# One-pass index products on stacked high and low parts in a one-core decoder step

## What is computed

```python
def _index_scores(qi, wi, ki):
    s = jnp.einsum('bthd,bsd->bths', qi.astype(jnp.float32), ki.astype(jnp.float32))
    scale = (IDX_DIM ** -0.5) * (IDX_HEADS ** -0.5)
    return jnp.einsum('bths,bth->bts', jax.nn.relu(s), wi.astype(jnp.float32)) * scale
...
def block(i):
    start = i * Q_BLOCK
    qib = lax.dynamic_slice_in_dim(qi, start, Q_BLOCK, axis=1)
    wib = lax.dynamic_slice_in_dim(wi, start, Q_BLOCK, axis=1)
    scores = _index_scores(qib, wib, ki)
    scores = jnp.where(causal[None], scores, -jnp.inf)
    _, idx = lax.top_k(scores, topk)
```

## Time and profile before

| | us |
|---|---|
| runs shown, median of 3 | 1151.43 |
| lowest, highest | 1148.69, 1152.35 |
| the profiled execution, its own time | 1152.24 |
| its span, first to last instruction | 1150.4 |
| TensorE busy | 1124.0 |
| VectorE, ScalarE, GpSimd busy | 641.1, 326.6, 374.1 |
| from the first index tile's matmuls to the first row score | 34.04 to 179.58 |

### The profile page before, as it was taken

The page is one execution under the profiler, slowest core; times in us unless marked ns, Lnnn a source line. Parts: engine busy times, 40 slices in busy tenths (PEclk is TensorE's granted clock), DMA queues, the critical chain, the costliest instruction groups (busy, mean ns, idle before and its releaser), DMA issues.

```text
span 1150.4 us, 29654 instructions
## 1 busy us (share of the span) xinstructions
PE 1124.0 (98%) x11836; PEld 1048.8 (91%) x11836; DVE 641.1 (56%) x1184; ACT 326.6 (28%) x605; POOL 374.1 (33%) x158
## 2 busy tenths in 40 slices
PE   7999999999999999999999999999999999999996
PEld 6888889999999999999999898988989889999994
DVE  3566667897547556754266564555546443233356
ACT  4333333323332322232232221221212332121340
POOL 1532332333234333433441313221322233433570
PEclk9999999999999999999999999999999999999997
DMA  8433242233233323335423888888978785232333
GB/s 264 121 102 88 81 103 75 77 102 84 74 93 100 81 81 92 84 83 167 116 61 116 279 307 283 308 280 275 331 244 298 224 289 139 73 91 81 105 108 156
DMA packets 208040, 175.87 MB, mean 153 GB/s; under 512 B 20114, under 2 KB 188874, under 8 KB 206706
## 3 DMA queue, kind: packets, MB, share of 16 engines
q1 hardware_dynamic: 194392, 165.58, 46.5%
q10 hardware_dynamic: 13538, 8.68, 2.7%
HBM read 164.29 MB, written 10.03 MB: 152 GB/s over the span
## 4 chain that ended last, share of the span: by engine, by line
PE 90%; DVE 5%; DMA 2%; issue 1%; SPq 0%; ACT 0%; DVEq 0%; ACTq 0%
PE acc L1180 66%; PE acc L1162 4%; PE acc L1595 3%; PE bank L1526 3%; PE bank L1281 2%; PE bank L1398 2%; PE acc L1648 2%; PE bank L1417 1%; DVE scoreP L1900 1%; PE acc L1252 1%; DMA xnat<-in_x_prompt 1%; DVE top L1896 1%; PE acc L1554 1%; PE bank L1333 1%; PE bank L1407 1%
## 5 line engine op out<-in xcount | busy, mean ns | idle before, releaser
L670 POOL TENSOR_TENSOR wL<-rawW,wH 128x1024 fp32r<-128x1024 f32 (+1 forms) x154 | 373.9, 2430 | 745.6 <-ACT wH L692 745.5
L1180 PE MATMUL acc<-actH,wH 128*128 128x272 f32 x2136 | 457.2, 295 | 0.0
L1180 PE MATMUL acc<-actH,wL 128*128 128x272 f32 x2136 | 441.9, 288 | 0.0
L1180 PE MATMUL acc<-actL,wH 128*128 128x272 f32 x2136 | 440.8, 288 | 0.0
L1180 PEld LDWEIGHTS acc<-actH,wH 128*128 128x128 f32 x2136 | 334.7, 188 | 30.1 <-issue 29.6
L1180 PEld LDWEIGHTS acc<-actL,wH 128*128 128x128 f32 x2136 | 335.8, 189 | 0.0
L1180 PEld LDWEIGHTS acc<-actH,wL 128*128 128x128 f32 x2136 | 333.8, 189 | 0.0
L692 ACT ACTIVATE wH<-rawW 128x1024 fp32r<-128x1024 f32 (+1 forms) x154 | 161.7, 1054 | 260.1 <-PE acc L1180 232.1
L1852 DVE SCALAR_TENSOR_TENSOR scoreP<-relu,wiN,scoreP 128x256 f32<-128x256 f32 (+2 forms) x54 | 45.4, 880 | 33.4 <-ACT relu L750 33.4
L2248 DVE SCALAR_TENSOR_TENSOR y<-y,bank 128x512 f32 x12 | 8.2, 688 | 89.0 <-PE bank L1715 87.0
L2005 DVE STREAM_TRANSPOSE kPage<-kPage 128x1024 f32<-128x1024 f32 x30 | 37.1, 1236 | 36.5 <-DMA kPage<-in_cache_k 35.8
(11 more groups left out here) (238 smaller groups left out, 1118.6 us busy)
## 6 DMA issues: line engine op xcount, KB each, us to landing
rawW<-in_w_in SPq DMA_DIRECT2D x112, 512.0 KB, 3.9
vPage<-in_cache_v SPq DMA_DIRECT2D x64, 512.0 KB, 6.9
kPage<-in_cache_k SPq DMA_DIRECT2D x60, 512.0 KB, 5.1
rawW<-in_w_out SPq DMA_DIRECT2D x40, 512.0 KB, 4.0
y<-in_x_prompt SPq DMA_DIRECT2D x4, 1024.0 KB, 7.8
out_y_prompt<-y SPq DMA_DIRECT2D x8, 512.0 KB, 2.7
xnat<-in_x_prompt SPq DMA_DIRECT2D x2, 1024.0 KB, 6.4
xnat<-in_x_prompt ACTq DMA_DIRECT2D x2, 1024.0 KB, 9.5
```

The source lines that it names most:

```text
L670: pool.tensor_tensor(wL[:, slot, :, 0:width], rawW[:, slot, :, 0:width], wH[:, slot, :, 0:width].bitcast(F32), ALU.subtract).then_inc(stag ...
L1180: last = pe.matmul(acc[t.slot][0:width, e, 0:HT], w[:, u.slot, k, 0:width], a[:, kk, e * HT:(e + 1) * HT], start=(half == 0 and k == 0 and ...
```

## The change

Three buffers are new: kiHigh and kiLow (128 x 512, the high and low part of the key on both halves of the rows) and qSplit (two slots, two heads, 384 columns), all float32r. For head 0 the high part of the query stands on rows 0 to 63 and the low part on rows 64 to 127; for head 1 it is the other way round. A product is now two matmuls with the same stationary queries on 128 rows, one against kiHigh and one against kiLow. ScalarE makes the high parts (split_high, two copies of 64 x 384 per tile), VectorE the low ones (two subtracts). The first, cleared set is gone: the loop runs three times, one set before it is empty, and tile 7's turn stands behind it with the names s and banks of its own (qb). The pairs of a set stand a quarter tile later. raw's copy moves ahead of products 2 and 3 on ScalarE and VectorE, the split ahead of 4 and 5, and so does the copy of tile C to raw in the last set.

```diff
+RA = 3 * 12
+RT = RA + 6
...
+            qSplit = sb("qSplit", [P, 2, 2, NP_ - P], F32R, s)
+            kiHigh = sb("kiHigh", [P, NP_], F32R, s)
+            kiLow = sb("kiLow", [P, NP_], F32R, s)
...
-        rb = banks.stage([*rt("r0"), *rt("r1")], four, 4)
+        rb = banks.stage([*rt("r0"), *rt("r1")], four, 3)
+        qb = banks.stage(rt("s"), four)
...
+            act.wait_ge(ki_twice, 16)
+            act.activation(kiHigh[:], kiT[:, 0:NP_], ACT.Copy).then_inc(ki_high, 1)
+            def split_high(a, i=None):
+                slot = a % 2
+                act.wait_ge(qi_ready, a + 1 if i is None else 2 * i + (a + 1))
+                act.activation(qSplit[0:ID, slot, 0, :], raw[0:ID, slot, P:NP_], ACT.Copy)
+                act.activation(qSplit[ID:P, slot, 1, :], raw[ID:P, slot, P:NP_], ACT.Copy).then_inc(qi_high, 1)
+            def index_tile(a, products, i=None):
+                per = 0 if i is None else 2
+                high(TILE_A + a + 2, 0, i, per)
+                for n, product in enumerate(products):
+                    if n == 2:
+                        src, copied = projected(TILE_A + a, i, per)
+                        act.activation(halves(raw[:, a % 2]), src, ACT.Copy).then_inc(copied, 1)
+                    if n == 4:
+                        high(TILE_A + a + 2, 1, i, per)
+                        split_high(a, i)
+                    rectify(*product)
...
             for n, name in enumerate(rt("z")):
+                if n == 4:
+                    copy_tile(0, raw[:, 0])
                 behind.append(zb(name))
                 rectify(zb(name), behind[n], (int(name[-1]) + 1) * P, P, turn(RT + n, 2))
-            copy_tile(0, raw[:, 0])
             high(TILE_C + 2, 1)
...
-                    full(b, pe.matmul(take(b)[:, 0:(t + 1) * P], raw[part, slot, t * P:(t + 1) * P],
-                                      kiT[part, 0:(t + 1) * P], start=True, stop=True))
+                    dst = take(b)[:, 0:(t + 1) * P]
+                    queries = qSplit[:, slot, e, (t - 1) * P:t * P]
+                    pe.matmul(dst, queries, kiHigh[:, 0:(t + 1) * P], start=True, stop=False)
+                    full(b, pe.matmul(dst, queries, kiLow[:, 0:(t + 1) * P], start=False, stop=True))
...
+            for tile in range(1, H):
+                unit(TILE_A + tile, 0, quarters=(0,))
+                if tile > 1:
+                    products(tile - 2, 4, 6)
+                unit(TILE_A + tile, 0, quarters=(1,))
                 unit(TILE_A + tile, 1, quarters=(0,))
-                products(2, 4)
+                if tile == 1:
+                    pe.wait_ge(ki_split, 1)
+                pe.wait_ge(qi_split, tile)
+                products(tile - 1, 0, 2)
                 unit(TILE_A + tile, 1, quarters=(1,))
-                products(4, 6)
+                products(tile - 1, 2, 4)
...
-            unit(TILE_C, 0)
+            unit(TILE_C, 0, quarters=(0,))
+            products(H - 2, 4, 6)
+            unit(TILE_C, 0, quarters=(1,))
             pe.wait_ge(kip_in, 16 * NB * PAGES)
...
-            pe.wait_ge(qi_ready, H + 1)
             names = rt("z")
+            unit(TILE_C, 1, quarters=(0,))
+            pe.wait_ge(qi_split, H)
             index_products(zb, names[0:2], 1)
-            unit(TILE_C, 1, quarters=(0,))
+            unit(TILE_C, 1, quarters=(1,))
             index_products(zb, names[2:4], 1)
-            unit(TILE_C, 1, quarters=(1,))
+            unit(TILE_C + 1, 0, quarters=(0,))
             index_products(zb, names[4:6], 1)
-            unit(TILE_C + 1, 0, quarters=(0,))
...
-            own.step(dve.memset(wiN[:, :, 0:2], 0.0))
-            dve.memset(raw[:, 1, :], 0.0).then_inc(qi_ready, 1)
...
+            dve.wait_ge(ki_high, 1)
+            dve.tensor_tensor(kiLow[:], kiT[:, 0:NP_], kiHigh[:].bitcast(F32), ALU.subtract).then_inc(ki_split, 1)
...
+                def split():
+                    dve.wait_ge(qi_high, at + 1)
+                    dve.tensor_tensor(qSplit[ID:P, slot, 0, :], raw[0:ID, slot, P:NP_],
+                                      qSplit[0:ID, slot, 0, :].bitcast(F32), ALU.subtract)
+                    dve.tensor_tensor(qSplit[0:ID, slot, 1, :], raw[ID:P, slot, P:NP_],
+                                      qSplit[ID:P, slot, 1, :].bitcast(F32), ALU.subtract).then_inc(qi_split, 1)
```

More of the change, by code:

```diff
@@ new lines, in index_tile @@
+            def index_tile(a, products, i=None):
[9 more added lines that the diff above has]
+                    rectify(*product)
+                if not products:
+                    src, copied = projected(TILE_A + a, i, per)
+                    act.activation(halves(raw[:, a % 2]), src, ACT.Copy).then_inc(copied, 1)
+                    high(TILE_A + a + 2, 1, i, per)
+                    split_high(a, i)
@@ L753, in _, with width @@
+            def width(name):
+                return (int(name[-1]) + 1) * P
+            index_tile(0, ())
+            with act.Fori(0, 3) as i:
                 names = rt("r0") + rt("r1")
                 for j in range(2):
[L755 to L761, removed]
@@ L762, in _ @@
-                    high(TILE_A + j + 2, 1, i, 2)
+                    index_tile(1 + j, [(rb(names[n], i), rb(names[n - 2], i) if n >= 2 else rb(names[n + 10], i, ago=1),
+                                        width(names[n]), P, turn(n, 2, i, 12)) for n in range(6 * j, 6 * j + 6)], i)
+            names = rt("s")
+            index_tile(7, [(qb(names[n]), qb(names[n - 2]) if n >= 2 else rb(rt("r1")[n + 4], 2),
+                            width(names[n]), P, turn(RA + n, 2)) for n in range(6)])
@@ L1853, in add_head, with index_tile, turned @@
                                          ).then_inc(bank_free[b.slot], 1)
-            with dve.Fori(0, 4) as i:
+            dve.wait_ge(ki_high, 1)
+            dve.tensor_tensor(kiLow[:], kiT[:, 0:NP_], kiHigh[:].bitcast(F32), ALU.subtract).then_inc(ki_split, 1)
+            def index_tile(a, products, i=None):
+                slot = a % 2
+                at = a if i is None else 2 * i + a
+                def turned():
+                    copied(TILE_A + a, i, 0 if i is None else 2)
+                    rotate(raw[:, slot], raw[:, slot], P, irot, SWAP_I).then_inc(qi_ready, 1)
+                def split():
[4 more added lines that the diff above has]
+                                      qSplit[ID:P, slot, 1, :].bitcast(F32), ALU.subtract).then_inc(qi_split, 1)
+                for n, product in enumerate(products):
+                    if n == 2:
+                        turned()
+                    if n == 4:
+                        split()
+                    add_head(*product)
+                if not products:
+                    turned()
+                    split()
+                own.step(dve.tensor_copy(qiN[:, ds(at, 1), :].rearrange("p a t -> p (a t)"), raw[:, slot, NP_:T]))
+            index_tile(0, ())
+            with dve.Fori(0, 3) as i:
                 own.enter(i, 8)
@@ L1858, in _ @@
                 for j in range(2):
[L1859 to L1868, removed]
+                    index_tile(1 + j, [(rb(names[n], i), rb(names[n - 3], i) if n >= 3 else rb(names[n + 9], i, ago=1),
+                                        int(names[n][-1]), turn(n, 2, i, 12), 4 * i + (2 * j + int(names[n][-2]) + 2))
+                                       for n in range(6 * j, 6 * j + 6)], i)
+                own.leave(3)
+            names = rt("s")
+            index_tile(7, [(qb(names[n]), qb(names[n - 3]) if n >= 3 else rb(rt("r1")[n + 3], 2), int(names[n][-1]),
+                            turn(RA + n, 2), 14 + int(names[n][-2])) for n in range(6)])
             own.wait()
@@ L1871, in _ @@
             dve.tensor_copy(qiS[ID:P, 1, 1:IH:2, :], qiN[ID:P]).then_inc(qis_near, 1)
-            behind = [rb(name, 3) for name in rt("r1")[-3:]]
+            behind = [qb(name) for name in rt("s")[-3:]]
             for n, name in enumerate(rt("z")):
```

33 lines of the change are left out of this document (14 added, 19 removed).

## The result

The changed kernel takes 1141.97 us (median of 6 runs, 1139.0 to 1142.58), the kernel before 1151.89 beside it (6 runs); the ratio is 0.991, 95% interval 0.9893 to 0.9926. That is 9.9 us less, inside the range of the prediction (1134.6 to 1142.5) but only 0.5 us under its upper end, 2.8 us over its point. The spans differ by the same 9.9 us: 1150.4 and 1140.5.

What follows compares the result with a forecast made beforehand. TensorE, busy 98% of the span, was taken to bound the kernel. Products save 16.15 us, new waits of 1.5 and 2.4 leave 12.25; against 1151.43 the forecast is 1139.2 us, range 1134.6 to 1142.5.

Steps and rivals of the forecast that it cites:

- Price of the old set: Index stage on TensorE: a tile's six old products cost 3.56 us, the cleared set at the start 3.81 us.
- Price of the new set: Index stage on TensorE: a set of 12 one-pass matmuls costs 2.06 us, between 1.92 and 2.7.
- Price of the last set: Stage of tile C on TensorE: the last set falls from 3.91 to 2.06 us, 1.85 less.
- The split in time: Each index tile: split ready 8.0 us after the tile's matmuls end (E), TensorE asks at 10.3, so no wait.
- The pages: SP's queue: the last 16 index pages land at about 149.4 us, 1.6 us before TensorE needs them, no price.
- First new wait: Page transposes: TensorE waits for the bank of the fifth product's add, 1.25 us plus 0.25, 1.5 in all.
- Second new wait: Row scores: VectorE multiplies meet GpSimd, TensorE waits 2.4 us for the third, 0.4 of it at the values' transposes.
- rival A: Row scores: the second new wait doesn't come, giving 1136.8 us; chance 0.24.
- rival B: Row scores: both new waits come and TensorE's clock falls on the second, 1.7 us lost, giving 1140.9 us; chance 0.22.
- C: End of the index stage: neither new wait comes, giving 1135.3 us; chance 0.08.
- D: Index tiles: the split is late in every tile and TensorE waits 2.6 us in seven, giving 1162 us; chance 0.04.
- E: Products on TensorE: a product's two matmuls are not one pass each, a set costs 8.8 us, giving 1189; chance 0.01.

Runs made afterwards that it cites:

- half: Changed kernel without the product with the key's low part, one matmul a product instead of two: 1134.36 us, ratio 0.9846.
- turned banks: Changed kernel with the bank order behind the index tiles turned by two, so the first page transposes take banks 6 and 7: 1139.62 us, ratio 0.9906.
- early: Changed kernel with the pairs of products of tiles 1 to 7 back at their old places: 1155.2 us, ratio 1.0038.
- both: Changed kernel with the turned banks and the second high part of tile C + 2 two relus earlier on ScalarE: 1141.75 us, ratio 0.9919.
- high: Changed kernel with the second high part of tile C + 2 two relus earlier on ScalarE: 1141.02 us, ratio 0.9925.
- again: The changed kernel itself, unchanged, profiled a second time: 1142.96 us, ratio 0.9928.
- cleared: Kernel before without its cleared set, products at old places, copy to raw and rotation ahead of products 2 and 3 in the loop: 1149.12 us, ratio 0.9986.

## Why the prediction was right, and where it was off

- **TensorE bounds the stage.** Right: a microsecond taken from the products left the stage whole (half: 8 sets of 1.09 less are 8.7 us, and 7.9 came off the stage; the bank's wait is 0.7 longer).
- **Price of the old set**, 3.56, and of the cleared one, 3.81. Right: 15.57 of pitch with the old products, 3.7 for the cleared set. One reading beside it was wrong: the four records of a pair don't start together. Two start at 87.42, the other two at 87.74 and 87.86; they overlap, and the pair's 0.92 us stands.
- **Price of the new set**, 2.06. Measured 2.13, 0.5 us more over seven tiles. The three widths start 0.12, 0.175 and 0.235 us apart, by columns and 12 to 22 ns, so the extra of one matmul that I took from 272 columns was too low for the widest.
- **Price of the last set.** The prediction took 3.91 - 2.06 = 1.85 us off. From the first of the key transposes to the first row score TensorE took 13.28 us before and takes 11.69 now, 1.6 less.
- **The split in time.** Right almost to the number. Predicted at E + 8.0; E is 143.9 and the second subtract ends at 151.99, E + 8.1. Copies 0.53 each (0.45 taken), subtracts 0.55 each (0.5):

```profile
149.78 0.53 ACT L769 ACTIVATE qSplit<-raw 64x384 fp32r<-64x384 f32 x1 [3.52 <-DVE raw L1869]
150.32 0.52 ACT L770 ACTIVATE qSplit<-raw 64x384 fp32r<-64x384 f32 x1
150.87 0.55 DVE L1911 TENSOR_TENSOR qSplit<-raw,qSplit 64x384 fp32r<-64x384 f32 x1
151.44 0.55 DVE L1913 TENSOR_TENSOR qSplit<-raw,qSplit 64x384 fp32r<-64x384 f32 x1
```

- **The pages.** Right: the last 16 land 1.8 us behind this, at about 149.6 (149.4 predicted); TensorE is there at 151.4.

```profile
123.58 24.21 SPq L489 DMA_DIRECT2D kiPage<-in_cache_kidx  x16
```

- **First new wait**, the bank: 1.25 + 0.25 predicted. The wait is 1.36, and the transposes last 1.23 instead of 0.87, so 1.7 together, and the turned banks show the cause:

```profile
152.79 1.23 PE L1353 MATMUL bank<-sq,kiPage 128*128 128x128 f32 x8 [1.36 <-DVE scoreP L1893]
```

- **Second new wait**, 2.4 predicted, of it 0.4 at the values' transposes. Measured 0.65 + 1.40 and, from the first to the third row score, 177.27 - 165.64 = 11.6 us against 9.2 before: 2.4. The size was right, but the step was wrong in two points. GpSimd met the causal adds, which the prediction had left out of VectorE's list: before, they were done 2.4 us ahead of the multiply. And the second meeting did not need the first, so rival A, which rested on "it needs two meetings", was less likely than its 0.24.
- **The sum.** 12.25 predicted, 11.1 in the stage: 0.5 for the price of the set, 0.3 for the last set, 0.2 for the bank, 0.1 for the cleared set and 0.1 for TensorE's start behind the wait at the third row score. The other 1.2 us, from 11.1 to 9.9, are in the rest, where the prediction's step "no more is added behind" took for granted that a lead carries. There TensorE was idle for 1.0 us more than before; but that idle time differs by 2.5 us between executions of the same instructions, so whether the change loses something there is **open**.
- **Luck.** The time is nearer to rival B's 1140.9 than to the forecast's 1139.2, though B's fall of the clock didn't happen. It lies inside the range because the upper end left room for such a fall or for a dearer set; neither came, and what took 2.3 of the 12.25 us is the small terms above and the 1.2 in the rest.
- **Rivals.** A and C are excluded by the waits, D by the split (early shows its mechanism at a lower price), E by the pitch. B didn't happen in the changed kernel; with such a wait the clock did fall in two others (both and early).

The Trainium skill's rule on the port (SBUF — State Buffer, SBUF: two separate sides), that a VectorE instruction with two SBUF inputs and a GpSimd instruction that reads SBUF exclude each other, is borne out: three causal adds that take 0.7 us together took 2.90, and a multiply that takes 0.7 took 2.82, both beside GpSimd. The Trainium skill's rule on row tiles (TensorEngine Tiling (Array Packing), Key Properties), that a change of tiling mode drains the array, fits the 6.21 us of 48 matmuls behind 64-row products and the 6.01 behind 128-row ones.

## What to carry over

Where TensorE bounds a stage, price products by the distance between starts, seams included: one pass on 128 rows from two stacked parts beat float32 on 64 rows, 2.13 us to 3.56, even though the old pairs overlapped. Follow every list that the change shortens: page transposes that came to take the banks of the pair just ahead of them, and a pair that came a quarter later, took back 4.1 us, about a quarter of the gain, and three edits of order returned 3.0 of it. Once a wait is explained by a meeting of two engines, look whether the next meeting is in reach; here each of two was enough, and an edit that removed one changed nothing.

## What was not expected of the hardware

- A VectorE copy with a single input, 128 x 32, which takes 0.17 us in all eight places before, takes 2.37 to 2.42 in seven of the eight in the changed kernel, each time beside GpSimd, while a TENSOR_REDUCE (1.09) and the MAX8 and MATCH_REPLACE8 instructions kept their times. With the old products in the new order seven of the eight stay at 0.17 to 0.18, so it is the new pitch that brings them under GpSimd; TensorE doesn't pay for it in the tiles, where it waits for nothing. One of them:

```profile
138.87 2.55 POOL L680 TENSOR_TENSOR wL<-rawW,wH 128x1024 fp32r<-128x1024 f32 x1 [3.85 <-ACT wH L702]
...
139.09 2.38 DVE L1925 COPY qiN<-raw 128x32 f32 x1
```

The Trainium skill counts a float32 copy within SBUF among the instructions that need the shared port (SBUF — State Buffer, SBUF: two separate sides); the row agrees.

- A wait of TensorE of about 2 us is no sure trigger of the lower clock: 2.23 us in two kernels, one with the fall behind it (both) and one without (high); 1.7 us at the same matmuls, with it at 628 us in again and without it at 634 in cleared; 1.8 us near 780, with it in the changed kernel and without it in again.
- With the same instructions, the first index matmul starts between 31.7 and 34.2 us and the rest of the kernel takes 941.5 to 945.8 us; a low stretch of the clock at about 19 us is in seven of the twelve profiles, and those start at 32.9 or later.
